# The first attention's output projection from rounded parts, and the last expert's rows centred in its slots

## The chip, the cores and the metric

One core of a Trainium2 chip runs the whole program in one launch. The metric is the device time of one execution in microseconds, the median over several runs. The engines are TensorE (PE; its weight loads are PEld), VectorE (DVE), ScalarE (ACT), GpSimd (POOL) and SyncE (SP, which here only issues transfers).

## What is computed

Two blocks of two layers each on 256 tokens of width 1024, all in fp32. The first layer of the first block is a sparse mixer: eight heads of block attention and eight heads of compressed, selected and windowed attention, whose outputs are joined and multiplied by a 1024 x 1024 matrix; then a gated feed-forward. The very last operation of the second block is a mixture of 8 experts, a residual sum and a layer norm. Cut to the two places that the change touches:

```
# first layer
o = jnp.concatenate([o_moba, o_nsa], axis=1)...reshape(B, S, SPARSE_OUT)   # 256 x 1024
y = o @ w_out                                                            # sp_w_out, 1024 x 1024
x = x + g_a * y
h = rms_norm(x, ffn_norm[i]) * (1.0 + sc_f) + sh_f
x = x + g_f * swiglu(h, ...)
...
# last layer
for e in range(N_EXPERTS):
    out = out + combine[:, e:e + 1] * swiglu_2(t, wg[e], wu[e], wd[e])
h = layer_norm(alpha * h + g2 * out, ln_g[l, 1], ln_b[l, 1])
```

A layer norm takes the mean over the 1024 channels off each token, divides by the deviation, and applies a gain and a shift.

## The kernel before

**Layout and order.** Activations lie channels by tokens: 8 tiles (`X[:, k, :]`, k = 0 to 7) of 128 channels x 256 tokens. There is no scheduler: the program of each engine is written out by hand as a list, and semaphores tie the lists together (`job.filled`, `job.emptied` for PSUM banks, counters such as `head_upper` for tiles). An engine works strictly in the order of its list, so an instruction that waits holds up all that stands behind it.

**Products of rounded parts.** Most large products are made three times over at the fast rate of the rounded fp32 type: ScalarE copies the weights rounded (the upper part), VectorE subtracts that from the weights in place (the remainder), and TensorE adds upper x upper, remainder x upper and upper x remainder. The first attention's output projection (`project_out(sp_out, sp_y, OT)`) is one of the few still made once, in plain fp32: 64 products of 128 x 256, each recorded as two.

**Units.** The attention runs as 24 units (`units(sp_units, ...)`, a unit is 128 query rows by 384 keys; the first 8 heads have one, the others two). For unit i TensorE makes scores, VectorE their greatest value (`nmax`), ScalarE the exponential and its sum, VectorE the factor (`work<-work,fac`), TensorE turns the result, ScalarE copies it, TensorE multiplies it with the values, and ScalarE copies a finished head to `OT`. In its iteration i ScalarE copies the turned unit i-2 and makes the exponential of unit i. Both `units` take a table `between` of things to do at the start of iteration i.

**Conditioning rows.** The scale, shift and gate of every layer come from `ada_w`, read as chunks of 1 MB into two buffers (`nring`). GpSimd issues a transfer (`load_rows`, L1173) when VectorE has used up the chunk two before it; VectorE multiplies and sums a chunk (`add_more`, L3046, two instructions of 128x1024 for each chunk, each followed by its accumulator). Behind the units VectorE has, in this order: chunks 6 to 8, the remainders of the first gate weights, chunks 9 to 11, the remainders of the first up weights (whose last rounding on ScalarE waits for chunk 11, as its buffer is a buffer of these rows), the factor `gsc`, and then the residual sums `X<-ps,mod,X` of the projection.

**Weights.** SyncE loads weights in 2 MB chunks into a ring of 6 slots, in order; a chunk waits until the chunk six before it is used up.

**The tail.** Expert 7's results (two PSUM banks, rows are slots of up to 128 tokens) are scaled by their gate, rounded and split (`results`), and spread from slots to tokens by 16 products with a table (`scatter`, the q-th quarter of the channels into bank `last_spread[q]`). VectorE adds each tile to X with the layer's gate (`add_residual`), ScalarE squares it, TensorE sums the squares. What the other experts gave was added and its mean taken off while the last expert ran (`centre`, 8 instructions), so the tail owes the mean of the last expert's part: the sum of the tiles (`rstd`), its product with ones, three small VectorE steps on `ncol`, and one more subtraction for each tile before the scaling. ScalarE then applies gain and shift, and SyncE stores pairs of tiles.

## Time and profile before

| | |
|---|---|
| median of 3 runs | 2221.87 us (2220.83 to 2222.57) |
| the profiled execution | 2224.2 us, its span 2222.3 us |
| granted TensorE clock | 0.996 of full |
| PE, DVE, ACT, POOL busy | 2176.0 (98%), 1852.4 (83%), 1335.8 (60%), 86.2 us (4%) |
| transfers | 633.33 MB, 285 GB/s on average |

The units of the first attention run up to 169 us into the span, the projection from 169.7 to 197.5 us, the first feed-forward from 202.7 us; the tail begins at 2201 us. A busy TensorE here does not mean that it is never waited for: in the stretches around the change other engines' lists end last.

### The profile page before, as it was taken

The page shows a single profiled execution, that of the slowest core. Times are in us where ns is not written, and L with a number is a line of the kernel's source. Part 1 is how long each engine was busy: PE and PEld are TensorE (multiplying, and loading weights), DVE is VectorE, ACT ScalarE, POOL GpSimd, SP SyncE. Part 2 cuts the span into 40 slices and gives each one's busy share as a digit, 9 for nine tenths or more (in the row PEclk, how much of TensorE's full clock was granted, in tenths as well). Part 3 has the DMA queues.
Part 4 walks back from the last instruction along what each step waited for, and adds up shares of the span by engine and source line. Part 5 has one row for each costly group of instructions (what it writes and reads, how often), then busy time and mean ns, then how long its engine had stood idle before and what let it go on. Part 6 is the DMA issues. An engine that isn't in the chain of part 4 may idle for free.

```text
span 2222.3 us, 32055 instructions
## 1 busy us (share of the span) xinstructions
PE 2176.0 (98%) x13109; PEld 1918.6 (86%) x13123; DVE 1852.4 (83%) x2332; ACT 1335.8 (60%) x1508; POOL 86.2 (4%) x140
## 2 busy tenths in 40 slices
PE   6999999999999999999999999999999999999998
PEld 4888999889999979999798888888888888888886
DVE  7867888876998677888896988888888988888897
ACT  3574433665343776434633877777767777777775
POOL 3000111000010000010000000000000000000000
PEclk9999999999999999999999999999999999999999
DMA  9845988625887616885553999999999999999991
GB/s 369 297 186 200 341 325 300 227 77 209 303 298 272 223 39 253 307 332 187 204 201 105 369 348 369 344 370 351 353 366 345 364 346 369 344 364 354 357 363 70
DMA packets 259218, 633.33 MB, mean 285 GB/s; under 512 B 9304, under 2 KB 21625, under 8 KB 258554
## 3 DMA queue, kind: packets, MB, share of 16 engines
q1 hardware_dynamic: 234554, 536.83, 66.4%
q0 software_dynamic: 24512, 94.38, 11.4%
q8 instruction: 107, 1.75, 0.3%
q14 instruction: 45, 0.37, 0.0%
HBM read 630.13 MB, written 1.05 MB: 284 GB/s over the span
## 4 chain that ended last, share of the span: by engine, by line
PE 83%; DVE 11%; DMA 3%; issue 2%; ACT 1%; SPq 0%; POOL 0%; ACTq 0%; DVEq 0%
PE ps L1225 81%; DVE wring_rounded L3019 3%; DMA aring<-in_ada_rows 3%; DVE aring L3046 2%; DVE work L3019 1%; PE ps L2284 1%; PE ps L1421 1%; DVE OT L3043 1%; DVE F L3026 1%; DVE X L3026 0%; DVE F L3019 0%; PE ps L1396 0%; ACT scr_rounded L2349 0%; ACT F_rounded L2349 0%; DVE work_rounded L3019 0%
## 5 line engine op out<-in xcount | busy, mean ns | idle before, releaser
L3019 DVE TENSOR_TENSOR wring_rounded<-wring,scr_rounded 128x2048 fp32r<-128x2048 f32 (+1 forms) x314 | 568.9, 1840 | 76.0 <-ACT scr_rounded L2349 75.9
L2349 ACT ACTIVATE scr_rounded<-wring 128x2048 fp32r<-128x2048 f32 (+1 forms) x314 | 480.0, 1554 | 194.9 <-PE ps L1225 131.4
L1225 PE MATMUL ps<-wring_rounded,OT_rounded 128*128 128x512 f32 (+1 forms) x1184 | 314.8, 390 | 2.7 <-DVE wring_rounded L3019 1.7
L1225 PEld LDWEIGHTS ps<-wring_rounded,OT_rounded 128*128 128x128 f32 x1184 | 220.1, 188 | 47.2 <-DVE wring_rounded L3019 2.3
L3046 DVE CUSTOM_DVE_ANT_0 aring<-aring,F,vec 128x1024 f32<-128x1024 f32 x152 | 187.9, 1283 | 34.2 <-DMA aring<-in_ada_rows 33.5
L3019 DVE TENSOR_TENSOR wring_rounded<-wring,H_rounded 128x2048 fp32r<-128x2048 f32 (+1 forms) x85 | 193.3, 2275 | 25.5 <-ACT H_rounded L2349 25.3
L3019 DVE TENSOR_TENSOR wring_rounded<-wring,aring_rounded 128x2048 fp32r<-128x2048 f32 x84 | 192.4, 2290 | 16.2 <-ACT aring_rounded L2349 16.2
L2349 ACT ACTIVATE H_rounded<-wring 128x2048 fp32r<-128x2048 f32 (+1 forms) x85 | 162.4, 1910 | 61.0 <-issue 39.5
L2349 ACT ACTIVATE aring_rounded<-wring 128x2048 fp32r<-128x2048 f32 x84 | 161.2, 1919 | 58.1 <-PE ps L1225 57.4
L1225 PE MATMUL ps<-V_rounded,wring_rounded 128*128 128x256 f32 x1184 | 177.9, 285 | 4.6 <-DVE wring_rounded L3019 4.6
L1225 PE MATMUL ps<-work_rounded,F_rounded 128*128 128x256 f32 x1056 | 169.8, 283 | 0.0
L1225 PEld LDWEIGHTS ps<-V_rounded,wring_rounded 128*128 128x128 f32 x1184 | 158.8, 192 | 7.7 <-DVE wring_rounded L3019 7.5
L1225 PE MATMUL ps<-V_rounded,scr_rounded 128*128 128x256 f32 x1056 | 159.4, 285 | 0.0
L1225 PE MATMUL ps<-H_rounded,scr_rounded 128*128 128x256 f32 (+1 forms) x1072 | 152.9, 286 | 0.0
L1225 PE MATMUL ps<-scr_rounded,OT_rounded 128*128 128x512 f32 x560 | 151.1, 394 | 0.1
L1225 PEld LDWEIGHTS ps<-work_rounded,F_rounded 128*128 128x128 f32 x1056 | 145.7, 192 | 0.0
L1225 PEld LDWEIGHTS ps<-V_rounded,scr_rounded 128*128 128x128 f32 x1056 | 142.9, 193 | 1.5 <-issue 1.1
L1225 PEld LDWEIGHTS ps<-H_rounded,scr_rounded 128*128 128x128 f32 x1072 | 139.3, 193 | 1.5 <-issue 1.0
L1225 PE MATMUL ps<-scr_rounded,F_rounded 128*128 128x512 f32 x464 | 124.9, 389 | 0.0
L1225 PEld LDWEIGHTS ps<-scr_rounded,OT_rounded 128*128 128x128 f32 x560 | 103.6, 188 | 22.3 <-issue 1.6
L1225 PE MATMUL ps<-wring_rounded,work_rounded 128*128 128x512 f32 x448 | 120.2, 390 | 0.0
L1225 PE MATMUL ps<-scr_rounded,work_rounded 128*128 128x512 f32 x448 | 114.0, 396 | 0.0
(366 smaller groups left out, 3728.2 us busy)
## 6 DMA issues: line engine op xcount, KB each, us to landing
wring<-in_moe_gate SPq DMA_DIRECT2D x56, 2048.0 KB, 8.1
wring<-in_moe_up SPq DMA_DIRECT2D x56, 2048.0 KB, 8.8
wring<-in_moe_down SPq DMA_DIRECT2D x56, 2048.0 KB, 8.2
aring<-in_ada_rows POOLq DMA_DIRECT2D x88, 1024.0 KB, 8.0
wring<-in_ffn_w_gate SPq DMA_DIRECT2D x10, 2048.0 KB, 10.7
wring<-in_ffn_w_up SPq DMA_DIRECT2D x10, 2048.0 KB, 14.5
wring<-in_ffn_w_down SPq DMA_DIRECT2D x10, 2048.0 KB, 10.3
wring<-in_diff_w_in SPq DMA_DIRECT2D x6, 2048.0 KB, 15.7
```

What stands on the lines that cost most here:

```text
L1225: return pe.matmul(dst, lhsT, rhs, start=start, stop=stop, **kw)
L1421: last = pe.transpose(PS[t[u].b][:, dst:dst + P], pr[:, src:src + P], C("ident"))
L2284: last = pe.transpose(PS[job.b][:, m * P:(m + 1) * P], act_buffer(q)[:, m * P:(m + 1) * P], C("ident"))
L2349: return act.activation(dst, src, ACT.Copy, **kw)
L3019: return ve.tensor_tensor(dst, x, y, op)
L3026: return ve.scalar_tensor_tensor(out=dst, in0=x, scalar=s, in1=y, op0=op0, op1=op1)
L3043: ve.tensor_tensor_reduce(OTl[:, m * D:(m + 1) * D], w[:, m, :], context, 1.0, vec[:, o + m:o + m + 1], ALU.mult, ALU.add, modc[:, first + ...
L3046: last = ve.tensor_tensor_reduce(w[:, m, :], w[:, m, :], row, 1.0, vec[:, o + m:o + m + 1], ALU.mult, ALU.add, mod[:, layer, first + m:fir ...
```

## The change

**The projection.** It is made in three products of rounded parts. ScalarE rounds the two weight chunks in eight pieces of 128x1024 at the start of its iterations 10, 12, ... 24 of the units (`round_sparse_out`, into two new ring slots `sp_out_hi` that are held until the projection's banks are full), and each pair of heads at the start of iterations 11, 13, 15, 17, 19, 21, 25 and once behind the units (`round_heads`, into F). GpSimd subtracts the rounded weights in place (`out_rest`, eight tensor_tensor of 128x1024), VectorE makes the remainders of the heads (`head_rest`, eight of 128x256): six in the units, the last two behind them and ahead of chunk 6. TensorE makes 192 products (`sparse_split`). GpSimd's load of the conditioning vector moves behind chunk 11's load and waits for the whole projection. Two semaphores are merged into one.

**The tail.** The layer's gate is written out as rows (`gate_rows`: PE products of a broadcast column with the identity in place of eight of the idle products around the routing, and two ScalarE copies). The last expert's slot gate moves into the product of its hidden rows (`egate` in seven instructions that were plain products). For the last expert `last_results` multiplies its results with the gate rows and sums them (two custom instructions with accumulator), takes the mean off each slot in the rounding itself, so nothing is owed after the spreading. GpSimd sums the other experts' tiles (7 additions) and takes their mean off (8 subtractions) in place of VectorE. In the tail VectorE adds each tile once and scales it once, and applies gain and shift to tiles 5 to 7, ScalarE to tiles 0 to 4.

The core of the diff:

```diff
+        sp_out_hi = [Chunk(ring, dmas=0) for _ in range(2)]
+        sp_out_hi[0].freed_by, sp_out_hi[1].freed_by = sp_y[1].when_full(), sp_y[4].when_full()
...
+            def out_rest():
+
+                pool.wait_ge(vrows_ready, 2)
+                for c in range(2):
+                    for q in range(4):
+                        pool.wait_ge(out_upper, 4 * c + q + 1)
+                        pool.tensor_tensor(quarter_weights(sp_out[c], q), quarter_weights(sp_out[c], q, False),
+                                           sp_out_part(c, q).bitcast(F32), ALU.subtract).then_inc(out_lower, 1)
+
             for n, c in enumerate(ada1):
                 if n == 8:
                     compressed_rows()
-                if n == EARLY - 1:
-                    condition_rows(sp_y, (0,))
+                    out_rest()
+                if n == EARLY:
+                    condition_rows(sp_y[4:], (0,))
                 load_rows(c, 0, 16 + 2 * n)
...
+            for r in range(1, KT):
+                if r in (1, 4):
+                    pool.wait_ge(x_tile, X_TILES[7] - (1 if r == 1 else 0))
+                if r > 1:
+                    pool.wait_ge(norm_sums, 9 + r - 1)
+                pool.tensor_tensor(rstd[:], X[:, 0, :] if r == 1 else rstd[:], X[:, r, :], ALU.add).then_inc(norm_sums, 1)
+            norm_job[7][0].emptied(pool)
+            for k in range(KT):
+                pool.tensor_tensor(X[:, k, :], X[:, k, :], rstd[:], ALU.subtract).then_inc(norm_sums, 1)
...
-            project_out(sp_out, sp_y, OT)
+
+            def sparse_split(dst, c, lo):
+
+                wu, wl = ([part(q).rearrange("p (k n) -> p k n", k=2) for q in range(4)] for part in (
+                    lambda q: sp_out_part(c, q), lambda q: quarter_weights(sp_out[c], q)))
+                for n, (x, w) in enumerate(((head_main, wu), (head_main, wl), (head_part, wu))):
+                    for k in range(KT):
+                        if c == 0 and lo == 0 and n != 1:
+                            pe.wait_ge(head_lower if n else head_upper, k + 1)
+                        if lo == 0 and n < 2 and k % 2 == 0:
+                            pe.wait_ge(out_lower if n else out_upper, 4 * c + k // 2 + 1)
+                        last = mm(dst, w[k // 2][:, k % 2, lo:lo + P], x[:, k, :], n == 0 and k == 0, n == 2 and k == KT - 1)
+                return last
+
+            project_out(sp_out, sp_y, OT, split=sparse_split)
...
-            idle_products(5, 10)
+            pe.wait_ge(ada_used, ADAS[3])
+            gate_rows(0)
+            idle_products(5, 5)
...
-            units(sp_units, sparse_specs(), 0, heads_to, 0, {1: last_values, 2: compressed_products, 6: compressed_exp, 9: compressed_turned})
+            def round_sparse_out(c, q):
+
+                if q == 0:
+                    sp_out[c].loaded(act)
+                    sp_out_hi[c].room(act)
+                copy(sp_out_part(c, q), quarter_weights(sp_out[c], q, False)).then_inc(out_upper, 1)
+
+            def round_heads(t):
+
+                for h in (2 * t, 2 * t + 1):
+                    sp_units[2][h].emptied(act)
+                copy(head_main[:, t, :], OT[:, t, :]).then_inc(head_upper, 1)
+
+            units(sp_units, sparse_specs(), 0, heads_to, 0,
+                  {1: last_values, 2: compressed_products, 6: compressed_exp, 9: compressed_turned}
+                  | {10 + 2 * n: lambda n=n: round_sparse_out(n // 4, n % 4) for n in range(8)}
+                  | {11 + 2 * t: lambda t=t: round_heads(t) for t in range(5)} | {21: lambda: round_heads(5), 25: lambda: round_heads(6)})
+            round_heads(7)
...
+            def last_results():
+
+                mj["s", NE - 2, 3].filled(act)
+                mj["y", NE - 1, 1].emptied(act)
+                for h in range(2):
+                    act.activation(ye_upper(h), last_y(h), ACT.Identity, bias=ymean[:, 0:1]).then_inc(ye_upper_made, 1)
+
+            norm_job[7][0].filled(act)
+            act.activation(rstd[:], PS[norm_job[7][0].b][:, 0:T], ACT.Copy, scale=1.0 / D).then_inc(norm_job[7][0].bank.free, 1)
             upper("d", LAST)
-            results(NE - 1)
+            last_results()
...
+            def head_rest(t):
+
+                ve.wait_ge(head_upper, t + 1)
+                tt(head_part[:, t, :], OT[:, t, :], head_main[:, t, :].bitcast(F32), ALU.subtract).then_inc(head_lower, 1)
+
+            units(sp_units, sparse_specs(), 0, {4: branch_gates, 5: compressed_shift, 7: compressed_weights}
+                  | {13 + 2 * t: lambda t=t: head_rest(t) for t in range(5)} | {23: lambda: head_rest(5)})
+            for t in range(6, KT):
+                head_rest(t)
...
-                tt(x, x, PS[job.b][:, :], ALU.mult).then_inc(job.bank.free, 1)
+                if q // GROUPS == NE - 1:
+                    mj["st", NE - 1].emptied(ve)
+                    e = (NE - 1) % 2
+                    stt(x, PS[job.b][:, :], egate[:, e:e + 1], x, ALU.mult, ALU.mult).then_inc(job.bank.free, 1)
+                else:
+                    tt(x, x, PS[job.b][:, :], ALU.mult).then_inc(job.bank.free, 1)
...
+            def last_results():
+
+                for h in range(2):
+                    job = mj["y", NE - 1, h]
+                    job.filled(ve)
+                    step(ve.tensor_tensor_reduce(last_y(h), PS[job.b][:, :], last_gate[:, h * CH:(h + 1) * CH], 1.0,
+                                                 ysum[:, 0:1] if h else 0.0, ALU.mult, ALU.add, ysum[:, h:h + 1]))
+                    if h == 0:
+                        ve.sem_inc(job.bank.free, 1)
+                ts(ymean[:], ysum[:, 1:2], -1.0 / D, ALU.mult).then_inc(job.bank.free, 1)
+                for h in range(2):
+                    ve.wait_ge(ye_upper_made, 2 * (NE - 1) + h + 1)
+                    stt(ye_lower(h), last_y(h), ymean[:, 0:1], ye_upper(h).bitcast(F32), ALU.add, ALU.subtract).then_inc(
+                        lower_made, 1)
+
             lower("d", LAST)
-            results(NE - 1)
-            norm_job[7][0].emptied(ve)
+            last_results()
             for k in range(KT):
-                add_residual(last_spread, 3, 40, k)
-                if k % 2:
-                    for r in range(k - 1, min(k + 1, KT - 1)):
-                        if r:
-                            tile_ready(ve, last_spread, X_TILES[7], r)
-                            ins = tt(rstd[:], rstd[:] if r > 1 else X[:, 0, :], X[:, r, :], ALU.add)
-                            if r < KT - 2:
-                                step(ins)
-            ins.then_inc(norm_sums, 1)
+                ve.wait_ge(norm_sums, LAST_SUMS + k + 1)
+                job, m = last_spread[k // 2], k % 2
+                job.filled(ve)
+                tt(X[:, k, :], X[:, k, :], PS[job.b][:, m * T:(m + 1) * T], ALU.add).then_inc(job.bank.free if m else x_tile, 1)
...
-            layer_norm(7)
-
+                norm_job[7][1].filled(ve)
+                for k in range(KT):
+                    over_step(stt(X[:, k, :], PS[norm_job[7][1].b][:, 0:T], -1.0 / D, X[:, k, :], ALU.mult, ALU.add))
+            inverse(7)
+            root = inverse_rows(7)
+            for k in range(KT):
+                tt(X[:, k, :], X[:, k, :], root, ALU.mult).then_inc(scaled, 1)
+            for k in range(LAST_BY_VECTOR, KT):
+                ve.wait_ge(scaled, KT * 7 + k + 1)
+                ts(X[:, k, :], X[:, k, :], vc("ln_g", 24 + k), ALU.mult, vc("ln_b", 24 + k), ALU.add).then_inc(x_tile, 1)
```

How the lists change at three places. ScalarE in the units, where the first weight piece and the first heads are rounded (`work<-ps` is the copy of a turned unit, `work,ssum<-work,nmax` an exponential, `OT<-ps` a finished head), before:

```order
L2349 ACTIVATE work<-ps 128x384
L2472 ACTIVATE work,ssum<-work,nmax 128x256
L2472 ACTIVATE work,ssum<-work,nmax 128x128
L2349 ACTIVATE OT<-ps 64x256
L2349 ACTIVATE work<-ps 128x384
L2472 ACTIVATE work,ssum<-work,nmax 128x256
L2472 ACTIVATE work,ssum<-work,nmax 128x128
L2349 ACTIVATE OT<-ps 64x256
L2349 ACTIVATE work<-ps 128x384
```

and of the change:

```order
L2414 ACTIVATE wring_rounded<-wring 128x1024
L2414 ACTIVATE work<-ps 128x384
L2538 ACTIVATE work,ssum<-work,nmax 128x256
L2538 ACTIVATE work,ssum<-work,nmax 128x128
L2414 ACTIVATE OT<-ps 64x256
L2414 ACTIVATE F_rounded<-OT 128x256
L2414 ACTIVATE work<-ps 128x384
L2538 ACTIVATE work,ssum<-work,nmax 128x256
L2538 ACTIVATE work,ssum<-work,nmax 128x128
L2414 ACTIVATE wring_rounded<-wring 128x1024
```

Each pair of iterations has one rounding of 128x1024 ahead of the copy and the exponential of its even unit, and one of 128x256 ahead of those of its odd one.

VectorE behind the last unit, up to the first instruction on chunk 6 (`aring,mod<-aring,vec`), before:

```order
L3280 RECIPROCAL fac<-ssum 128x2
L3019 TENSOR_TENSOR fac<-fac,gates 128x2
L3022 TENSOR_SCALAR work<-work,fac 128x256
L3022 TENSOR_SCALAR work<-work,fac 128x128
L3046 ISA aring,mod<-aring,vec 128x1024
L3046 ISA mod 128x1
```

and of the change:

```order
L3381 RECIPROCAL fac<-ssum 128x2
L3120 TENSOR_TENSOR fac<-fac,gates 128x2
L3123 TENSOR_SCALAR work<-work,fac 128x256
L3123 TENSOR_SCALAR work<-work,fac 128x128
L3120 TENSOR_TENSOR OT_rounded<-OT,F_rounded 128x256 x2
L3147 ISA aring,mod<-aring,vec 128x1024
L3147 ISA mod 128x1
```

The remainders of heads tiles 6 and 7 stand between the last factor and chunk 6; the second waits for `round_heads(7)`.

VectorE at the end of the program, from the last branch on, before (the first of its rows; six more pairs like the last two follow):

```order
L4026 UNCONDITIONAL_BRANCH
L3022 TENSOR_SCALAR ncol<-ps 128x2
L3019 TENSOR_TENSOR ncol<-ncol 128x2
L3019 TENSOR_TENSOR ncol<-ps,ncol 128x2
L3026 SCALAR_TENSOR_TENSOR X<-ps,X 128x256
L3218 RECIPROCAL ncol<-ncol 128x2
L3026 SCALAR_TENSOR_TENSOR X<-ps,X 128x256
L3019 TENSOR_TENSOR X<-X,ps 128x256
L3026 SCALAR_TENSOR_TENSOR X<-ps,X 128x256
```

and of the change:

```order
L4144 UNCONDITIONAL_BRANCH
L3210 RECIPROCAL ncol<-ncol 128x2
L3120 TENSOR_TENSOR X<-X,ps 128x256 x8
L3123 TENSOR_SCALAR X<-X,vec 128x256 x3
L320 UNCONDITIONAL_BRANCH
```

The three small steps on `ncol` and the second pass over X are gone; three tiles get gain and shift here.

## Rows read from the trace of the kernel before

**Rows 1.** Windows: stretch, length, busy us of PE, PEld, DVE, ACT, POOL; clock; DMA
```profile
148.67:164.45 15.78, 15.59 (x97) 13.91 (x96) 11.45 (x67) 12.53 (x44) 0.00 (x0) 1.00 0.00 1
```

**Rows 2.** Tile OT, and rounded products (start, length, engine, line, operation)
```profile
L1225 PE MATMUL ps<-OT,wring x128: 379/379/483, 169.7 to 197.2; 128*128 128x256 f32 x128
...
304.29 1.12 PE L1225 MATMUL ps<-H_rounded,scr_rounded 128*128 128x256 f32 x8
305.25 1.12 PE L1225 MATMUL ps<-V_rounded,scr_rounded 128*128 128x256 f32 x8
```

**Rows 3.** Timeline of ScalarE, two close pieces of the units
```profile
129.29 0.49 ACT L2349 ACTIVATE work<-ps 128x384 f32<-128x384 f32 x1
...
130.55 0.37 ACT L2349 ACTIVATE OT<-ps 64x256 f32<-64x256 f32 x1
...
140.63 0.38 ACT L2349 ACTIVATE OT<-ps 64x256 f32<-64x256 f32 x1
141.04 0.49 ACT L2349 ACTIVATE work<-ps 128x384 f32<-128x384 f32 x1
```

**Rows 4.** Timeline of ScalarE, roundings and squares back to back
```profile
169.64 2.95 ACT L2349 ACTIVATE scr_rounded<-wring 128x1024 fp32r<-128x1024 f32 x3
...
194.01 1.59 ACT L2367 ACTIVATE H<-X 128x256 f32<-128x256 f32 x4 [0.37 <-DVE X L3026]
```

**Rows 5.** Timeline of all engines, end of the units to the feed-forward
```profile
166.71 1.28 DVE L3046 CUSTOM_DVE_ANT_0 aring<-aring,vec 128x1024 f32<-128x1024 f32 x1
...
169.24 0.38 ACT L2349 ACTIVATE OT<-ps 64x256 f32<-64x256 f32 x1 [1.25 <-PE ps L1225]
...
169.50 0.72 POOL L1173 DMA_DIRECT2D aring<-in_ada_rows  x1 [33.83 <-DVE mod L3046]
...
174.78 1.28 DVE L3046 CUSTOM_DVE_ANT_0 aring<-aring,vec 128x1024 f32<-128x1024 f32 x1 [3.17 <-DMA aring<-in_ada_rows]
...
193.29 0.16 DVE L3026 SCALAR_TENSOR_TENSOR gsc<-mod,vec 128x8 f32<-128x8 f32 x1
...
198.02 0.87 DVE L3026 SCALAR_TENSOR_TENSOR X<-ps,mod,X 128x256 f32<-128x256 f32 x2
...
202.69 0.47 PE L1225 MATMUL ps<-V_rounded,scr_rounded 128*128 128x256 f32 x1
```

**Rows 6.** Windows of one microsecond (columns as in Rows 1), and products in one
```profile
310.00:311.00 1.00, 0.46 (x3) 0.46 (x4) 1.00 (x2) 1.00 (x3) 0.00 (x0) 1.00 1.07 399
312.00:313.00 1.00, 1.00 (x7) 1.00 (x6) 1.00 (x2) 1.00 (x2) 0.00 (x0) 0.50 1.04 414
...
312.51 1.91 PE L1225 MATMUL ps<-H_rounded,scr_rounded 128*128 128x256 f32 x8
```

**Rows 7.** Timelines of GpSimd and VectorE, and the tile OT again
```profile
133.82 0.52 POOL L1196 MEMSET F<- 128x512 f32 x1 [22.36 <-PE ps L1648]
...
133.70 1.06 DVE L3022 TENSOR_SCALAR work<-work,fac 128x256 f32<-128x256 f32 x2
...
166.24 0.55 DVE L3022 TENSOR_SCALAR work<-work,fac 128x256 f32<-128x256 f32 x2
...
L1215 POOL TENSOR_TENSOR H<-OT x7: 612/612/692, 481.3 to 502.3; 128x256 f32<-128x256 f32 x7
```

**Rows 8.** Tail: timelines of ScalarE and VectorE, one piece of the chain
```profile
2201.16 0.69 ACT L2964 ACTIVATE F_rounded<-ps,egate 128x512 fp32r<-128x512 f32 x1 [0.67 <-PE ps L1225]
2202.35 1.28 ACT L3000 ACT_TABLE_LOAD   x1 [0.51 <-issue]
...
2209.31 2.90 PE ps L1225 x20
...
2212.82 0.30 ACT L2353 ACTIVATE ncol<-ncol,con 128x2 f32<-128x2 f32 x1 [3.17 <-DVE ncol L3019]
...
2214.18 0.42 DVE L3019 TENSOR_TENSOR X<-X,ps 128x256 f32<-128x256 f32 x1 [0.55 <-PE ps L1225]
...
2218.61 1.09 ACT L2356 ACTIVATE X<-X,vec 128x256 f32<-128x256 f32 x2
```

More of the change, by code:

```diff
@@ L718, in summed @@
         def summed(n, what="square"):
-            return n if n < 4 else {4: 3, 6: 6, 7: 9}[n] + ("shift", "dev", "square").index(what) + 1
+            return n if n < 4 else {4: 3, 6: 6}[n] + ("shift", "dev", "square").index(what) + 1
         def centred_tile(eng, n, k):
@@ L995, in build, with last_y @@
         spare = work[:, 2560:2816]
+        last_gate = aring[:, 0, 2048:3072]
+        def last_y(h):
+            return work[:, h * CH:(h + 1) * CH]
         def spread_sel(e):
@@ L2289, in scatter @@
                 job.open(pe)
-                if q == 0:
+                if e == NE - 1 and q % 2 == 0:
+                    pe.wait_ge(lower_made, REMAINDERS + q // 2 + 1)
+                elif q == 0:
                     mj["y", e, 1].emptied(pe)
@@ L2873, in _, with gate_rows @@
                 copy(V[:, n * 512:(n + 1) * 512], PS[zt_job[n].b][:, :]).then_inc(zt_job[n].bank.free, 1)
+            def gate_rows(h):
+                job = gate_job[h]
+                job.filled(act)
+                copy(last_gate[:, h * CH:(h + 1) * CH], PS[job.b][:, :]).then_inc(job.bank.free, 1)
+            gate_rows(0)
             def experts(M):
@@ L3002, in _ @@
             deviation(7)
-            for k in range(KT):
+            for k in range(LAST_BY_VECTOR):
                 act.wait_ge(scaled, KT * 7 + k + 1)
@@ L4003, in _ @@
                     ve.wait_ge(x_next, 3)
-                    step(add_experts(range(4)))
+                    add_experts(range(4)).then_inc(x_tile, 1)
                 if e + 1 == NE and s == 4:
-                    step(add_experts(range(4, KT)))
-                    tt(rstd[:], X[:, 0, :], X[:, 1, :], ALU.add).then_inc(norm_sums, 1)
-                if e + 1 == NE and s == 5:
-                    norm_job[7][0].filled(ve)
-                    for k in range(KT):
-                        centre(7, k)
+                    add_experts(range(4, KT)).then_inc(x_tile, 1)
```

102 lines of the change are left out of this document (57 added, 45 removed).

## The prediction

> **What bounds the kernel now.** I read the windows first, then the timelines of the two places that the change touches, then the chain of waits. TensorE is busy for 98% of the span, so one is tempted to count its instructions. At both places that would mislead. In the units of the first attention TensorE really sets the pace: over eight units it is busy for 15.59 of 15.78 us, VectorE for 11.45, ScalarE for 12.53 [rows 1]; the reader should note how little room ScalarE has. In the projection TensorE is busy too, from 169.7 to 197.6 us [rows 2], but what the feed-forward waits for is VectorE's list. It starts on conditioning chunk 6 at 166.71, waits 3.17 us for chunk 8, whose transfer GpSimd could only issue at 169.50, when half of the buffers was used up, reaches `gsc` at 193.29, and adds the last pair of X tiles at 198.02 with no idle time ahead of it, while TensorE had its last product ready by then [rows 2, 5]. The first product of the feed-forward is at 202.69. In the tail everything after the last product is one chain.
>
> **The projection, TensorE.** Removed: 128 records of 64 products, 169.7 to 197.2 + 0.4, 27.9 us. Added: 192 rounded products; eight of them take 305.25 - 304.29 = 0.96 us, so 0.12 each and 23.0 us in all [rows 2]. TensorE is done 4.9 us sooner. I count that as 0, because what comes next waits for VectorE's list; if that cover were gone it would be worth up to 4.9 us.
>
> **The units, ScalarE.** Added: a rounding of 128x1024 in every even iteration from 10 to 24 and one of 128x256 in most odd ones. Three roundings of 128x1024 took 2.95 us and the last of a row keeps its full 1.06, so about 0.95 each; four squares of 128x256 took 1.59, so 0.40 each [rows 4]. A pair of units lasts 15.78 / 4 = 3.95 us [rows 1]. What ScalarE needs for a pair when nothing holds it: 1.26 from a copy to the head behind it (129.29 to 130.55), twice, and 0.41 for the head (140.63 to 141.04), 2.93 us [rows 3]. With the roundings 2.93 + 0.95 + 0.40 = 4.28: ScalarE becomes the bound by 0.33 us a pair, 2.3 us over seven pairs (iterations 10 to 23). Behind the last exponential the rounding of iteration 24 and the heads' of 25 stand ahead of the last copy, 1.35 us, of which some 0.65 fall into time in which ScalarE now waits: 0.7. Sum 3.0. Lower bound 0 (the roundings fit into the waits after all); upper bound by busy time instead of starts, 12.53 / 4 + 1.35 = 4.48 a pair, 0.53 x 7 + 1.35 = 5.1. I take 3.0, since starts are what a full engine goes by.
>
> **Behind the units, VectorE.** The remainder of tile 7 waits until the last head is copied (169.24 + 0.38) and rounded (0.42 from one square's length, a 128x256 on this engine), and itself takes 0.42, the length of VectorE's 128x256 row in the tail [rows 4, 5, 8]. So chunk 6 starts at 169.62 + 0.42 + 0.42 + two handovers, about 170.5, instead of 166.71: 3.8 us. Nothing hides it. Queued behind the waiting instruction are the twelve conditioning instructions, and through them GpSimd's transfers, whose issue follows VectorE (169.50) and whose landing VectorE waits for (174.78) [rows 5]. The delay of 3.8 goes through whole to `gsc` and to the feed-forward. The lower bound is 0 (if those waits swallowed it), which the 1:1 tie of issue and use speaks against.
>
> **Ring and queues.** Two slots are held by the rounded weights until the projection's banks are full, so four later loads start some tens of us later and one of them beside chunk 10 or 11. Those two transfers may land up to 2 us later or 1 us sooner than now (their present wait is of the size of 3 us [rows 5]); I take 0. The late weights have two groups of the feed-forward before they are used.
>
> **The clock.** TensorE now has nothing for some 8 us between the end of the projection and the sums of squares. Where it last had such gaps, busy for 0.46 of a microsecond at 310, the granted clock fell to 0.50 of full (1.2 of 2.4 GHz), and eight products took 1.91 us instead of 1.12 [rows 2, 6]. The sums, the spread and the idle products ahead of the feed-forward would run at the low level; they span 198.02 to 202.69, of which half is TensorE's [rows 5]. I take 1.3 us, between 0 and 3.
>
> Sum of the first place: 0 + 3.0 + 3.8 + 0 + 1.3 = +8.1 us.
>
> **GpSimd's part there.** Eight subtractions of 128x1024. Its 128x256 took 0.61 us [rows 7]; by elements 2.45, less if part of it is fixed, so at most 20 us in all, spread over 28: off the path. But it has a side effect. Two factors of VectorE (`work<-work,fac`) take 0.55 us, and 1.06 when GpSimd's memset of 0.52 falls beside them (133.70 and 133.82) [rows 7]: VectorE stands still until GpSimd is through. The Trainium skill has the rule ("SBUF — State Buffer", section "Who interferes with whom"): GpSimd and VectorE share a port pair that one instruction holds to its end, against fast-mode VectorE instructions and, where GpSimd reads, against those with two inputs in SBUF. This trace agrees for the first kind. The skill's figure for GpSimd's tensor_tensor ("GPSIMD Engine Reference", 4497 ns for 2048 elements) would make 2.25 us of each, an estimate that leaves the sum as it is. I count 0: ScalarE copies a turned unit two iterations, a whole pair of 4.28 us, after its exponential, so a factor that is 1 or 2 us late is still in time, and GpSimd starts about when one factor has just been made. See the second rival.
>
> **Around the routing.** Eight idle products go, eight small fp32 ones and two ScalarE copies come; both fall into waits. +0.1.
>
> **The tail.** Sooner or later than now:
> - The results of the last expert are full at 2201.16 [rows 8]. VectorE's product with its sum (no row has it; the nearest of that width is ScalarE's 0.69; I take 0.8 with the accumulator) and the mean 0.2: 2202.15. ScalarE's two roundings 1.25: 2203.4. Then what now starts at 2202.35: the load of the root's table, 1.28 us, which is at present hidden beside the spreading and now is not; with the 0.5 of issue before it and 0.2 behind, squares begin at 2205.3. They are eight by 0.40: 2208.5 [rows 4, 8]. VectorE's eight additions fit beside them.
> - TensorE's last sums end 0.6 later, 2209.1, against 2209.31 + 2.90 = 2212.21 now [rows 8].
> - Root, inverse and spread are 2214.18 - 2212.82 = 1.36 [rows 8]: scaling starts at 2210.5, 3.7 sooner.
> - Scaling: eight products of 0.42, some 0.34 apart, then three gain-and-shift instructions that I take at 0.25 (two factors of 256 and 128 columns take 0.55 [rows 7]): 3.6 us, end at 2214.1. Now ScalarE ends at 2218.61 + 1.09 = 2219.70 [rows 8]. Gain 5.6 us, and the store behind it is the same.
> Bounds: 4.5 if the sum with accumulator or the wait for GpSimd costs more, 6.5 if the table load stays hidden in part. I take 5.5. The seven products with `egate` and GpSimd's 15 instructions lie beside TensorE's last 40 us, where VectorE loses 2.7 us of its own work.
>
> **Sum.** 8.1 + 0.1 - 5.5 = +2.7 us on the profiled execution (span 2222.3, 2224.2 with what lies around it); the median of the runs is 2.3 less than that execution, so 2221.87 + 2.7 = 2224.6.
>
> **The rivals.**
> 1. The projection's 4.9 us are kept and neither ScalarE nor VectorE gets late: faster. For it speaks that TensorE is the busiest engine at both places; against it the row at 198.02 without idle time. It decides if chunk 6's start moves less than 1 us. -4.9 - 5.5: 2211.5.
> 2. GpSimd's lock stalls the units: each of eight subtractions holds a factor up by 1 us that TensorE then waits for. For it speaks 1.06 instead of 0.55; against it those two iterations. It decides once a subtraction lasts beyond about 3 us, half as long again as its parts suggest, or meets both factors of a pair. +8 more: 2232.5. It is the Trainium skill's rule carried to its end.
> 3. ScalarE fits its roundings in, only VectorE's hold remains and the clock stays up: 3.8 - 5.5 = -1.6 with the routing: 2220.3.
> 4. The tail gains only half (a mean that waits for GpSimd's last subtractions, the table load): 2227.4.
>
> **How the numbers follow.** A change under 0.2% (4.4 us) can't be told from none here. Forecast 0.55, own range 2220 to 2229.5; rivals 0.10, 0.15, 0.12, 0.08. Slower than 2226.3: the second rival, most of the fourth, and 0.3 of the forecast: 0.36. Faster than 2217.4: the first and a little of the third and of the forecast, 0.14. The rest 0.50. The range leaves out the first rival and half of the second: 2217 to 2231.5.
>
> **What would show it.** The windows of the units: ScalarE nearly full, TensorE no longer, and the projection's first product at 173 instead of 169.67. VectorE idle ahead of chunk 6, released by ScalarE, and 6.8 us later than 166.71. TensorE idle for about 8 us behind the projection, a clock of 0.5 after it, the first feed-forward product near 211. In the tail a table load that ends last before the squares, scaling 3.7 us sooner, and 5.5 us less from the last product to the end. The prediction is wrong if the projection starts within 1 us of now, if chunk 6 does, or if factors of over 1.5 us stand beside GpSimd's subtractions.

## The result, and the profile after

2241.85 us (median; 2239.46 to 2242.01), against 2221.87: ratio 1.0086, 95% interval 1.0072 to 1.0099, so 0.9% slower. I had forecast 2224.6 and a range from 2217 to 2231.5. The profiled execution has a span of 2237.5 us, 15.2 more than before. The medians are 20.0 apart: the profiled execution of the kernel before is 2.3 above its median, that of the change 2.4 below. What follows accounts for the 15.2.

The windows of the same stretch of the units as in [rows 1], same columns:

```profile
148.67:164.45 15.78, 9.78 (x60) 8.65 (x59) 14.07 (x43) 10.79 (x35) 6.96 (x3) 1.00 0.01 1
```

TensorE fell from 15.59 to 9.78 us of 15.78, and ScalarE, which I took for the new bound, is less busy than before (10.79). VectorE is at 14.07, and much of that is time in which it is held, not work. The timeline of one place in it, GpSimd and VectorE, then TensorE, which waits:

```profile
154.37 2.35 POOL L1230 TENSOR_TENSOR wring_rounded<-wring,wring_rounded 128x1024 fp32r<-128x1024 f32 x1 [3.43 <-ACT wring_rounded L2414]
154.48 2.25 DVE L3120 TENSOR_TENSOR fac<-fac,gates 128x2 f32<-128x2 f32 x1
...
156.76 0.55 DVE L3123 TENSOR_SCALAR work<-work,fac 128x256 f32<-128x256 f32 x2
...
157.46 0.52 PE L1467 MATMUL ps<-con,work 128*128 128x128 f32 x3 [2.14 <-DVE work L3123]
157.56 0.42 DVE L3370 CUSTOM_DVE_ANT_0 work<-ps,con 128x256 f32<-128x256 f32 x1
```

A product of 128x2 elements lasts 2.25 us instead of 0.16: it starts 0.11 us after GpSimd's subtraction of 2.35 us and ends with it (156.73 and 156.72). Each of the eight subtractions has such a partner. In order they take 1.03, 1.17, 2.50 (`work<-work,fac`), 2.25 three times, 0.97, and 1.59 (the remainder of a head); without a subtraction beside them they take 0.16, 0.28 and 0.42. That is 12.3 us of stretching. TensorE waits 2.14 for the factor here, and ScalarE 1.90 for TensorE.

Behind the units, in the order of [rows 5] (timelines of TensorE, VectorE, GpSimd, SyncE's queue):

```profile
181.83 1.34 PE L1264 MATMUL ps<-F_rounded,wring_rounded 128*128 128x256 f32 x9 [0.47 <-ACT OT L2414]
...
182.32 0.43 DVE L3120 TENSOR_TENSOR OT_rounded<-OT,F_rounded 128x256 fp32r<-128x256 f32 x1 [0.82 <-ACT F_rounded L2414]
182.66 1.28 DVE L3147 CUSTOM_DVE_ANT_0 aring<-aring,vec 128x1024 f32<-128x1024 f32 x1
...
193.64 0.37 SPq L1035 DMA_DIRECT2D wring<-in_ffn_w_down  x1
...
193.64 0.72 POOL L1192 DMA_DIRECT2D aring<-in_ada_rows  x1 [5.06 <-DVE mod L3147]
...
204.02 1.28 DVE L3147 CUSTOM_DVE_ANT_0 aring<-aring,vec 128x1024 f32<-128x1024 f32 x1 [5.99 <-DMA aring<-in_ada_rows]
...
211.25 0.16 DVE L3127 SCALAR_TENSOR_TENSOR gsc<-mod,vec 128x8 f32<-128x8 f32 x1
...
216.11 2.88 PE L1264 MATMUL ps<-con,H 128*128 128x96 f32 x12 [10.76 <-DVE H L3120]
...
222.36 0.47 PE L1264 MATMUL ps<-V_rounded,scr_rounded 128*128 128x256 f32 x1
```

The projection starts 12.2 us later than before (predicted 3.0), chunk 6 15.9 later (12.2 + 3.8), `gsc` 18.0 later: another 2.0, because chunk 10's transfer is issued at the same instant as 2 MB of down weights, and VectorE waits 5.99 us for it. Before, it waited 1.05 for chunk 10 and 3.01 for chunk 11; the second wait is gone. The first product of the feed-forward is 19.7 later. The windows there, columns as in [rows 1] (clock third from the end):

```profile
210.00:215.00 5.00, 0.00 (x0) 0.00 (x0) 4.89 (x12) 3.97 (x9) 0.01 (x1) 0.54 0.99 370
215.00:220.00 5.00, 3.89 (x15) 3.07 (x16) 1.95 (x6) 1.07 (x3) 0.00 (x0) 0.50 1.03 407
```

The tail, against [rows 8]: results, squares, last sums, scaling, last tile, and the windows of the stores:

```profile
2219.32 0.75 DVE L4126 CUSTOM_DVE_ANT_0 work<-ps,aring,ysum 128x512 f32<-128x512 f32 x1 [0.66 <-PE ps L1264]
...
2223.30 2.73 ACT L2432 ACTIVATE H<-X 128x256 f32<-128x256 f32 x8
2227.99 0.26 ACT L2418 ACTIVATE ncol<-ps,con 128x2 f32<-128x2 f32 x1 [1.96 <-PE ps L1264]
...
2229.74 2.74 DVE L3120 TENSOR_TENSOR X<-X,ps 128x256 f32<-128x256 f32 x8 [0.86 <-PE ps L1264]
2232.40 1.05 DVE L3123 TENSOR_SCALAR X<-X,vec 128x256 f32<-128x256 f32 x3
...
2234.00:2235.00 1.00, 0.00 (x0) 0.00 (x0) 0.00 (x0) 0.00 (x0) 0.00 (x0) 0.50 1.03 381
2235.00:2236.00 1.00, 0.00 (x0) 0.00 (x0) 0.00 (x0) 0.00 (x0) 0.00 (x0) 0.50 0.25 88
2236.00:2237.00 1.00, 0.00 (x0) 0.00 (x0) 0.00 (x0) 0.00 (x0) 0.00 (x0) 0.50 0.04 16
```

From the full results (2219.32) to the end it is 18.2 us, before 2222.3 - 2201.16 = 21.1: a gain of 3.0 where I had 5.5. The last tile is finished at 2233.45, 4.05 us ahead of the end; before, 2219.70 was 2.6 ahead of it. The four stores are bunched, and the DMA engines are full for a while, at 381 GB/s; but in the last 2 us hardly anything moves. The last store lands 3.6 us after its issue (2233.52 to 2237.11), where before it took 2.2 (2219.72 to 2221.91).

### The profile page after: what moved, and what is told of

The parts are those of the page before. It is cut to its first block, busy times and chain, and to the rows that moved or that the text cites. A ratio compares the mean times of both kernels' runs of the same rounds, so it can differ in the third digit from the quotient of the medians.

```text
span 2237.5 us, 32229 instructions
## 1 busy us (share of the span) xinstructions
PE 2172.4 (97%) x13179; PEld 1918.0 (86%) x13179; DVE 1862.2 (83%) x2322; ACT 1344.0 (60%) x1524; POOL 132.6 (6%) x163
## 3 DMA queue, kind: packets, MB, share of 16 engines
q8 instruction: 107, 1.75, 0.3%
HBM read 630.13 MB, written 1.05 MB: 282 GB/s over the span
## 4 chain that ended last, share of the span: by engine, by line
PE 81%; DVE 12%; DMA 4%; issue 2%; ACT 1%; SPq 0%; DVEq 0%; ACTq 0%
PE ps L1264 78%; DMA aring<-in_ada_rows 4%; DVE wring_rounded L3120 3%; DVE aring L3147 3%; DVE work L3120 1%; PE ps L2346 1%; PE ps L1467 1%; DVE OT L3144 1%; DVE F L3127 1%; DVE fac L3120 0%; DVE work L3123 0%; DVE F L3120 0%; PE ps L1442 0%; DVE work_rounded L3120 0%; ACT F_rounded L2414 0%
## 6 DMA issues: line engine op xcount, KB each, us to landing
wring<-in_ffn_w_down SPq DMA_DIRECT2D x10, 2048.0 KB, 10.7
```

## The experiments

Times are to be read against a kernel before of 2222.1 (points 1 to 3), 2222.3 (points 4 to 7) and 2221.7 (points 8 and 9), the median that was measured along with them. "Run 2" is the run of point 2, and so on.

**1. The two parts apart.** The tail of the change alone, and the projection alone (the diff's hunks of the one part on the kernel before).

> The kernel before with the tail part of the change alone (centring of the last expert's rows, GpSimd's sums and subtractions, five tiles by ScalarE and three by VectorE); the projection is as before. If the two traces are read rightly, the tail is worth about 3.0 us (18.2 us from the last results to the end where the kernel before took 21.1): 2218.9, that is 0.9986 of the kernel before. If my predicted 5.5 was right and something that the projection part shifts ate the rest, 2216.4. If the tail's new work beside the experts (VectorE's seven products with the gate, GpSimd's 15 instructions) costs as much as it gives, no change.

Measured: 2219.5 (ratio 0.9988, 0.9978 to 0.9997), 2.65 below.

> The kernel before with the projection part alone (three products of rounded parts, ScalarE's and GpSimd's work in the units, VectorE's remainders of the heads); the tail is as before. From the traces: +12.2 us at the start of the projection, +3.8 of VectorE's hold, +2.0 at a transfer, +1.7 of clock and -1.5 in the feed-forward: +18.2, or 2240.1, and +15 to +23 with what the medians add to the profiled executions. Rival: the two parts cost each other something (the median of the change stands 20.0 above, its profiled execution 15.2), then this run is below +15.

Measured: 2243.3 (1.0094, 1.0077 to 1.0111), 21.2 above; span 2241.5, 19.2 more than before. Its units are those of the change (TensorE 9.78 us of 15.78). +21.2 and -2.65 make +18.5, the change has +20.0: the parts add up within their intervals, and all of the loss lies in the projection part.

**2. GpSimd's subtraction cut short.**

```diff
-   pool.tensor_tensor(quarter_weights(sp_out[c], q), quarter_weights(sp_out[c], q, False),
-                      sp_out_part(c, q).bitcast(F32), ALU.subtract)
+   pool.tensor_tensor(quarter_weights(sp_out[c], q)[:, 0:16], quarter_weights(sp_out[c], q, False)[:, 0:16],
+                      sp_out_part(c, q)[:, 0:16].bitcast(F32), ALU.subtract)
...
-   lambda q: sp_out_part(c, q), lambda q: quarter_weights(sp_out[c], q)))
+   lambda q: sp_out_part(c, q), lambda q: sp_out_part(c, q)))
```

> The change with GpSimd's eight subtractions cut from 128x1024 to 128x16; the second of the three products takes the rounded weights a second time in place of their remainders, so the remainders are left out of the result. Everything else stands, ScalarE's roundings too. Theory (GpSimd's instruction of 2.35 us shuts VectorE out): the units fall back to what ScalarE needs, a pair of 4.3 us at most, the projection starts at 170 to 173 instead of 181.8, and the time is 9 to 12 us below the change: 2230 to 2233. Rival A (ScalarE's roundings are the cost): the projection still starts at 181 to 182 and the time stays at 2241.8. Rival B (the fallen clock of TensorE in the units holds the pairs): half of it, 2236.

Measured: 2231.3, 10.6 below the change. Windows, VectorE's factors, the projection's first product, and the last remainder of a head:

```profile
148.67:164.45 15.78, 15.25 (x93) 13.40 (x93) 12.07 (x65) 15.64 (x52) 1.20 (x4) 1.00 0.00 1
...
L3120 DVE TENSOR_TENSOR fac<-fac,gates x8: 160/161/163, 149.8 to 164.5; 128x2 f32<-128x2 f32 x8
...
172.25 2.17 PE L1264 MATMUL ps<-F_rounded,wring_rounded 128*128 128x256 f32 x16 [0.47 <-ACT OT L2414]
...
172.74 0.43 DVE L3120 TENSOR_TENSOR OT_rounded<-OT,F_rounded 128x256 fp32r<-128x256 f32 x1 [1.99 <-ACT F_rounded L2414]
```

With the same roundings on ScalarE the projection starts at 172.25, 2.6 us later than before where I had said 3.0, ScalarE is busy for 15.64 of 15.78 us, and VectorE waits 1.99 for it ahead of the last remainder. So that part of the prediction describes this kernel. The other 9.6 us of the delay come with GpSimd's eight instructions and go with them. Rival A falls. Rival B can't be what holds the pairs: the granted clock is 1.00 in the stretch in which TensorE is busy for only 9.78 of 15.78 us. The fallen clock is a smaller part of the 9.6, sized further down.

**3. The same subtraction in four pieces.**

```diff
+   for s in range(4):
+       part = slice(256 * s, 256 * s + 256)
+       last = pool.tensor_tensor(quarter_weights(sp_out[c], q)[:, part], quarter_weights(sp_out[c], q, False)[:, part],
+                                 sp_out_part(c, q)[:, part].bitcast(F32), ALU.subtract)
+   last.then_inc(out_lower, 1)
```

> The change with each of GpSimd's eight subtractions in four pieces of 128x256 (some 0.6 us each), the same work in all. Theory that one instruction holds the shared port from its start to its end: VectorE gets in between two pieces, no factor waits longer than 0.6 us, pairs of 4.3 to 4.9 us, the projection starts at 171 to 175 and the time is 2232 to 2236. Rival C (what counts is GpSimd's total time at the port, or its traffic in SBUF): four pieces of 0.6 us block as one of 2.4, pairs stay at 6.0 and the time at 2241.8. Rival A as in the run before: no change.

Measured: 2233.7, 8.1 below the change, with the same arithmetic. GpSimd's four pieces and the factors:

```profile
152.99 3.02 POOL L1232 TENSOR_TENSOR wring_rounded<-wring,wring_rounded 128x256 fp32r<-128x256 f32 x4 [1.40 <-ACT wring_rounded L2417]
...
L3123 DVE TENSOR_TENSOR fac<-fac,gates x15: 160/161/635, 139.0 to 171.4; 128x2 f32<-128x2 f32 x15
...
148.67:164.45 15.78, 13.35 (x79) 11.37 (x79) 15.21 (x54) 14.76 (x46) 10.88 (x15) 1.00 0.00 1
...
175.25 2.17 PE L1267 MATMUL ps<-F_rounded,wring_rounded 128*128 128x256 f32 x16 [0.47 <-ACT OT L2417]
```

GpSimd is now busy for longer, 10.88 us of 15.78 instead of 6.96, and the units are 6.6 us shorter: most of the cost goes by the length of one instruction, not by the sum. The longest factor product is 0.64 us. Rival C falls. The projection starts at 175.25, still 3.0 later than with hardly any subtraction, so that much stays even in pieces.

**4. GpSimd writes only.** Each subtraction becomes `pool.memset(quarter_weights(sp_out[c], q, False), 0.0)`.

> The change with GpSimd's eight subtractions replaced by eight memsets of 128x1024 (by its 0.52 us for 512 columns about 1.04 each), which write and read nothing; as with the short subtraction, the second product takes the rounded weights again, so the remainders are left out. What it tells: whether GpSimd's reading matters. If the port is held against two-input VectorE instructions only by an instruction of GpSimd that reads, the product fac<-fac,gates keeps its 0.16 us beside a memset while work<-work,fac is stretched to as much as 1.3; if any GpSimd instruction holds up any of VectorE's, fac<-fac,gates shows up to 1.1 too. In both cases a pair stays near 4.2 us, and the time near 2231.

Measured: one time, 2230.3. On the small product the run says nothing: no memset fell beside one. It does say something on another instruction with two inputs in SBUF, the remainder of a head. Each memset began 0.06 to 0.12 us after ScalarE's rounding had ended (144.90 for the one at 144.96), and six of the eight began 0.10 or 0.11 us after such a remainder. VectorE's and GpSimd's rows of run 4, then GpSimd's of run 2, where a subtraction of 128x16 falls at the same place (its remainder begins at 148.27):

```profile
144.85 0.42 DVE L3119 TENSOR_TENSOR OT_rounded<-OT,F_rounded 128x256 fp32r<-128x256 f32 x1
...
144.96 0.95 POOL L1230 MEMSET wring<- 128x1024 f32 x1 [3.41 <-ACT wring_rounded L2413]
...
148.41 0.36 POOL L1230 TENSOR_TENSOR wring_rounded<-wring,wring_rounded 128x16 fp32r<-128x16 f32 x1 [3.65 <-ACT wring_rounded L2414]
```

The remainders keep their 0.42 and the memsets their 0.95, the length of those with no such partner (140.61 and 169.85). The subtraction, which reads, takes 0.36 or 0.37 beside a remainder in six cases and 0.22 without one in the other two. So in this pairing, in the one profiled execution of each run, GpSimd's reading is what makes the two meet.

**5. VectorE's hold.** On run 3:

```diff
-   for t in range(6, KT):
-       head_rest(t)
-   for n in range(6, 9):
-       add_more(n)
+   add_more(6)
+   head_rest(6)
+   add_more(7)
+   head_rest(7)
+   add_more(8)
```

> Based on the run with the subtraction in four pieces (2233.7, span 2231.7): VectorE takes conditioning chunk 6 ahead of the remainder of head tile 6, and chunk 7 ahead of that of tile 7, so that it does not stand waiting for ScalarE with the conditioning list behind it. There it stood 1.22 and 1.99 us. Theory (my term of 3.8 us is real and goes through to the feed-forward): chunk 8 can be added 3.0 us sooner, the time is 2.5 to 3 lower: 2231. Rival: from 195 to 220 the DMA engines are at 0.96 to 1.04 of their share with 361 to 407 GB/s, the chunks land no sooner, and the time stays at 2233.7.

Measured: 2235.9, 2.1 more than run 3, and neither theory said so. VectorE, GpSimd and TensorE:

```profile
171.90 1.28 DVE L3150 CUSTOM_DVE_ANT_0 aring<-aring,vec 128x1024 f32<-128x1024 f32 x1
...
173.10 1.74 DVE L3150 CUSTOM_DVE_ANT_0 aring<-aring,vec 128x1024 f32<-128x1024 f32 x1
...
200.91 1.28 DVE L3150 CUSTOM_DVE_ANT_0 aring<-aring,vec 128x1024 f32<-128x1024 f32 x1 [6.74 <-DMA aring<-in_ada_rows]
...
171.94 6.06 POOL L1232 TENSOR_TENSOR wring_rounded<-wring,wring_rounded 128x256 fp32r<-128x256 f32 x4 [1.41 <-ACT wring_rounded L2417]
177.94 0.74 POOL L1192 DMA_DIRECT2D aring<-in_ada_rows  x1
...
179.48 0.39 PE L1267 MATMUL ps<-OT_rounded,wring_rounded 128*128 128x256 f32 x1 [1.33 <-DVE OT_rounded L3123]
```

VectorE starts chunk 6 at 171.90 instead of 176.08, 4.2 us sooner, but now beside GpSimd's last subtraction: the two hold each other up. Its sums last up to 1.76 instead of 1.28, the last four pieces of GpSimd 6.06 instead of 2.96, and since GpSimd must issue chunk 8's load behind them, it does so only 0.9 us sooner (177.94 for 178.87). Chunk 8 is there 0.8 sooner, TensorE waits 1.33 for the last remainder, and chunk 11 comes late (6.74). `gsc` is 0.6 later than in run 3, the first product of the feed-forward 1.2. So this order doesn't give the hold back, while GpSimd is both subtracting and issuing; what the time would be without the hold, no run shows.

**6. The transfers.** On run 3, `sp_out[0].freed_by = sp_y[4].when_full()`, so that the down weights are loaded 11.6 us later.

> Based on the run in four pieces: the first 2 MB of the feed-forward's down weights are loaded only when the whole projection is through, 11 us later, so that they do not share the DMA engines with conditioning chunk 10, for which VectorE waits 5.81 us there (3.01 in the kernel before). Theory (the two transfers collide): the wait falls to 3 to 3.5 us and the time by 2 to 2.5, 2231.5. Rival: the chunk is late because of its own issue, nothing changes at chunk 10 (2233.7). Risk: the down weights come late for the second group of the feed-forward, and the time rises.

Measured: 2232.2, 1.6 below run 3. Chunks 10 and 11:

```profile
192.18 1.28 DVE L3151 CUSTOM_DVE_ANT_0 aring<-aring,vec 128x1024 f32<-128x1024 f32 x1 [0.91 <-DMA aring<-in_ada_rows]
...
196.93 1.28 DVE L3151 CUSTOM_DVE_ANT_0 aring<-aring,vec 128x1024 f32<-128x1024 f32 x1 [2.25 <-DMA aring<-in_ada_rows]
...
201.70 0.16 DVE L3131 SCALAR_TENSOR_TENSOR gsc<-mod,vec 128x8 f32<-128x8 f32 x1
```

The waits of 5.81 and 0.66 become 0.91 and 2.25, and `gsc` comes 3.4 us sooner (205.06 in run 3): the collision is shown. (The 3.01 that the expectation gives for chunk 10 in the kernel before is chunk 11's wait.) Of the 3.4, 2.6 are left at the first product of the feed-forward and 1.8 at the tail. That its weights now come later is a likely reason for the last part, and not shown apart.

**7. The clock.** On run 3, `idle_products(6, 44)` behind `project_out`.

> Based on the run in four pieces: 44 idle products of 512 columns (about 9.4 us) between the projection and the sums of squares, where TensorE has nothing for 10.7 us and its granted clock falls to 0.50. Theory (my term for the clock, 1.3 forecast, 1.7 by the two traces): granted clock stays at 1.00, the first product of the feed-forward comes 1.7 us sooner, 2232.0. Rival: VectorE and ScalarE set the pace there, and the products cost nothing and give nothing; 2233.7.

Measured: 2232.2, also 1.6 below run 3. The sums, which took 2.88 us in one piece in the change, and the first scaled tiles (215.12 in run 3):

```profile
209.84 0.69 PE L1267 MATMUL ps<-con,H 128*128 128x96 f32 x4 [1.47 <-DVE H L3124]
...
213.26 3.22 DVE L3131 SCALAR_TENSOR_TENSOR H<-X,gsc,ps 128x256 f32<-128x256 f32 x8 [0.94 <-PE ps L1267]
```

With products of no use TensorE keeps a granted clock of 1.00, and what follows is 1.9 us sooner.

**8. Both, and half of the work beside the projection.** Run 8a has both edits of 6 and 7. Run 8b on top of it leaves only the first chunk of weights to the units, every other pair; ScalarE rounds the second chunk behind the last head, and VectorE subtracts it:

```diff
+   def second_rest(q):
+       ve.wait_ge(out_upper, 4 + q + 1)
+       tt(quarter_weights(sp_out[1], q), quarter_weights(sp_out[1], q, False),
+          sp_out_part(1, q).bitcast(F32), ALU.subtract).then_inc(out_lower, 1)
+   add_more(6)
+   add_more(7)
+   ve.wait_ge(out_lower, 4)
+   for q in range(3):
+       second_rest(q)
+   add_more(8)
+   second_rest(3)
```

> The subtraction in four pieces, with the down weights loaded later and the idle products behind the projection, both at once. Each alone gave 2232.2 against 2233.7. If the two costs lie one behind the other (transfer, then clock), they add up: 2230.6, with granted clock 1.00 behind the projection and chunk 10's wait about 1. If one hides the other, 2232.

> As both_fixes, but only the first chunk of weights is rounded and subtracted in the units (every other pair); the second chunk's four roundings go to ScalarE behind the last head, and its four remainders to VectorE, mostly into its wait ahead of conditioning chunk 8. Theory (GpSimd's subtractions and ScalarE's roundings each cost the units about 3 us for eight): the projection starts 2 to 3 us sooner than 175.3, 172.5 to 173.5, VectorE loses at most 1.6 outside, and the time is 1 to 3 below both_fixes: 2228 to 2229.5. Rival: VectorE's four remainders (1.2 us each) push its list as far as the units gain, no change. It does not reach the kernel before (2222) in either.

Measured: 8a 2230.7 (1.0035, 1.0021 to 1.0048), so the two add up; 8b 2228.7 (1.0028, 1.0019 to 1.0037), 2.0 less, with an interval that overlaps 8a's. 8b's projection starts at 174.03 for 175.48 in 8a, later than the 172.5 to 173.5 that I had expected. VectorE's own four remainders took 1.2 us each, three of them in the time in which it waited for chunk 8. Even so the kernel is slower than before.

**9. The tail's stores.** The tail alone, first with `LAST_BY_VECTOR = 8` (all tiles by ScalarE), then with stores of 1, 2, 2, 2 and 1 tiles.

> The tail alone (2219.5, span 2216.7), with all eight gain-and-shift instructions on ScalarE, 0.51 each, and none on VectorE: the last is through about 0.9 us later, but the stores are spaced. From the traces the end of the program comes 4.0 to 4.3 us after the last tile where the stores are bunched and the DMA engines full (381 GB/s), and 2.6 after it in the kernel before. Theory (the store takes back what the three VectorE tiles gain): the end moves by -0.5 to +0.3. Rival (the last tile's own time counts): +0.9.

> The tail alone with the output stored in five pieces of 1, 2, 2, 2 and 1 tiles in place of four of 2, so that the DMA engines start half a microsecond sooner and have 128 KB instead of 256 behind the last tile. Theory (the end is set by the stores' traffic): 0.3 to 0.7 us less than the tail alone, 2219.0. Rival (a fixed time from the last issue to the end, 0.6 us of issue for each store): no change, or 0.3 more.

Measured: 2218.7 and 2218.7 (both 0.9983, 0.9974 to 0.9992), 0.8 below the tail alone, with intervals that overlap it; each against its own kernel before, it is 3.0 where the tail alone has 2.65. VectorE's timeline in the tail alone, scaling and its three last tiles:

```profile
2208.67 2.74 DVE L3071 TENSOR_TENSOR X<-X,ps 128x256 f32<-128x256 f32 x8 [0.87 <-PE ps L1246]
2211.33 1.05 DVE L3074 TENSOR_SCALAR X<-X,vec 128x256 f32<-128x256 f32 x3
```

The same with all gain and shift on ScalarE, VectorE's scaling and ScalarE's eight tiles:

```profile
2207.89 2.74 DVE L3071 TENSOR_TENSOR X<-X,ps 128x256 f32<-128x256 f32 x8 [0.87 <-PE ps L1246]
...
2208.35 4.04 ACT L2389 ACTIVATE X<-X,vec 128x256 f32<-128x256 f32 x8 [2.04 <-DVE X L3071]
```

From the start of scaling to the last tile it is 3.7 us with VectorE's help and 4.5 without; to the end of the span it is 2216.7 - 2208.67 = 8.0 and 2216.1 - 2207.89 = 8.2. The finer stores give 2216.5 - 2208.55 = 7.95, and the kernel before had 8.1 with a last tile 5.5 us after the start. So tiles that are ready sooner hardly bring the end nearer. That the first of these spans is smaller than the tail alone's lies ahead of the edit, in where scaling starts (0.8 sooner).

## Why the prediction was wrong

Point by point, sizes in us of the profiled executions:

| step | predicted | measured |
|---|---|---|
| units, ScalarE's roundings | +3.0 | +2.6 (run 2) |
| units, GpSimd's lock | 0 | +9.6 (change less run 2) |
| VectorE's hold ahead of chunk 6 | +3.8 | +3.8 |
| transfers | 0 | +2.0 |
| clock behind the projection | +1.3 | +1.7 |
| feed-forward to the tail | 0 | -1.5 |
| tail | -5.5 | -3.0 |
| sum | +2.7 with the routing | +15.2 |

**The step that failed** is "I count 0: ScalarE copies a turned unit two iterations, a whole pair of 4.28 us, after its exponential, so a factor that is 1 or 2 us late is still in time". I took the slack from the order of the code. The timeline of the kernel before has it, VectorE's factors and TensorE's transposes of them, two units of a pair:

```profile
151.37 0.55 DVE L3022 TENSOR_SCALAR work<-work,fac 128x256 f32<-128x256 f32 x2
...
152.06 0.52 PE L1421 MATMUL ps<-con,work 128*128 128x128 f32 x3
...
153.00 0.55 DVE L3022 TENSOR_SCALAR work<-work,fac 128x256 f32<-128x256 f32 x2
...
154.16 0.49 PE L1421 MATMUL ps<-con,work 128*128 128x128 f32 x3
```

One unit of each pair has 0.14 us of slack (151.92 to 152.06), the other 0.6 (153.55 to 154.16); neither has 4.28. And the row maxima of the next unit stand behind the factor on VectorE in any case (157.56 in the change). The subtractions fall on the units with 0.14: in the change TensorE starts 0.14 or 0.15 us after each of the seven stretched factors has ended (157.31 and 157.46), with the same form of transposes as at 152.06. Its waits ahead of them are 1.07, 0.67, 1.73, three times 2.14, and 0.85, together 10.7 us. In run 2 its waits for a factor sum to 2.6, so 8.2 of the 9.6 are waits. Most of the rest is the clock. TensorE's timeline in the change, after the last wait of 2.14:

```profile
169.53 0.87 PE L1467 MATMUL ps<-con,work 128*128 128x128 f32 x3 [2.14 <-DVE work L3123]
...
173.26 0.49 PE L1467 MATMUL ps<-con,work 128*128 128x128 f32 x3
```

The granted clock was 0.50 in the windows from 170 to 172. From one of these groups to the next it is 3.73 us; the same products took 2.10 at a clock of 1.00 (163.49 to 165.59). So the clock, which fell behind the waits, costs 1.6, and the two make 9.8 by this estimate against 9.6.

The second rival had the mechanism and a chance of 0.15, but I had priced it at 1 us each, from a memset of 0.52 us beside a factor. That its 8 us in all lie near the 9.6 is luck: a subtraction cost TensorE up to 2.14, others less, and 1.6 of the 9.6 is the clock. Its point of decision was wrong too: it needed a subtraction beyond 3 us or both factors of a pair, and 2.35 us on one small product sufficed. That product, of two inputs in SBUF, was in no term of mine; I looked at the factors alone.

The Trainium skill has the mechanism in "SBUF — State Buffer", section "Who interferes with whom": a VectorE instruction with two SBUF inputs contends with a GpSimd instruction that reads SBUF, and not with one that only writes it. This trace agrees with the first half, with 2.25 us for 128x2 elements beside 2.35 us; and run 4 beside run 2 agrees with the second, for the remainders of the heads. The same section has the port pair as a lock that is held for the whole instruction; runs 2 and 3 agree that the time of one instruction counts. The estimate of 2.25 us for 128x1024, from the Trainium skill's "GPSIMD Engine Reference", section "3.1 Elementwise — side-by-side cycle accounting", was near the 2.35 of the trace.

**The transfers** I took at 0 out of -1 to +2; it was the upper end, and run 6 shows the mechanism. **The tail** was off by 2.5. Scaling starts 1.1 later than the 2210.5 that I had said (2229.74 less the 18.16 by which the results are later, 2211.6), since TensorE's last sums end 1.9 us behind the last square and not 0.6, and root, inverse and spread take 1.75 and not 1.36 (2227.99 to 2229.74), while the squares end 0.6 sooner than I had. The other 1.45 is the store: "the store behind it is the same" was wrong, with a last landing 3.6 us behind its issue instead of 2.2. In the kernel before, the change and the three kernels with the tail alone, the end is 7.8 to 8.2 us behind the start of scaling, with a last tile 3.7 to 5.5 us behind it. Why, no run shows: the DMA engines are full for only a part of that time (shares of 1.03, 0.25 and 0.04 in the last three windows of the change). **What held**: the projection's 4.9 us of TensorE did not show (23.3 us for 23.0 predicted, with 10.8 of idle time behind it), the hold of 3.8 (chunks 6 and 9 are both 16 us later than before, so nothing up to there hid it), and the fall of the clock to 0.50. That the -1.5 in the feed-forward is the stall of [rows 6] that is gone as a drop in clock I only read from the traces.

**What is open**: what a memset does beside the small product; what sets the end behind the stores; and why 8b's units are only 1.4 shorter than 8a's with half of the subtractions. TensorE's waits for a factor sum to 4.6 us there for 5.5 in 8a: they are fewer, but longer ones.

The faster version is the tail alone, 2219.5, below both kernels; with either edit of run 9 it is 2218.7, which these runs don't tell apart from it.

## What to carry to other kernels

Before work is given to GpSimd beside a tight loop, look in the timeline for every VectorE instruction that can fall beside it, the smallest with two SBUF inputs above all, and for how long its result lies before it is used. The price of one GpSimd instruction is about its length less that slack (here 2.35 less 0.14, and TensorE waited 2.14), so cut it into pieces as short as they can be made at little cost. Read slack from two rows of the trace, for each unit of a pair by itself, not from the distance of iterations in the code. And at the end of a program count up to the landing of the last store: here a last tile that was made 0.8 us sooner behind the start of scaling brought the end only 0.2 nearer.

## What the runs showed of the hardware

A VectorE product of 128x2 took 2.25 us beside a GpSimd subtraction of 2.35 and 0.16 alone. GpSimd's subtraction of 128x1024 took 2.35 us, and four of 128x256 2.8 to 3.1 together. A memset of 128x1024 took 0.95 and left a remainder of a head, with two SBUF inputs, at its 0.42 (run 4); a subtraction of 128x16 took 0.36 beside one and 0.22 without (run 2). It goes the other way too: in the change an addition of 128x256 by GpSimd, 0.61 us elsewhere [rows 7], took 4.91 beside two of VectorE's subtractions that ran back to back for 4.49.

GpSimd's timeline, then VectorE's, in the change:

```profile
2178.93 4.91 POOL L1255 TENSOR_TENSOR rstd<-X 128x256 f32<-128x256 f32 x1 [1125.03 <-DVE X L3127]
...
2178.76 4.49 DVE L3120 TENSOR_TENSOR wring_rounded<-wring,scr_rounded 128x2048 fp32r<-128x2048 f32 x2
```
